# Moving the output gate's products from the stick-breaking heads into the mLSTM heads

## The reference, cut to what matters

```
q_sb, k_sb, v_sb, qk_ml, v_ml, o_ml, i_ml, f_ml = jnp.split(h @ w_in, cuts)
y_sb = rms_norm_2(stick_breaking(q_sb, k_sb, v_sb), g_out_sb)
y_ml = rms_norm_2(mlstm(q_ml, k_ml, v_ml, i_pre, f_pre), g_out_ml) * sigmoid(o_ml)
x = x + gate1 * (concat(y_sb, y_ml) @ w_out)
x = x + gate2 * peer(h2, ...)          # 128 experts per token, gathered rows
```

## Time and profile before

| | |
|---|---|
| median of three runs | 2725.64 us |
| the profiled execution, its time | 2722.03 us |
| its span | 2720.3 us |
| busy PE / DVE / ACT / POOL | 2202.9 / 1785.0 / 632.5 / 786.2 us |
| last values of stick-breaking end, half 0 / half 1 | 754.1 us / 1750.1 us |
| mLSTM from its first matmul to its last result, half 0 / half 1 | 754.9 to 776.2 us / 1750.9 to 1780.7 us |

### The profile page before, as it was taken

How to read it: one execution, slowest core, us unless ns; L and a number is a source line. 1 busy time by engine, 2 the same in 40 slices (tenths; PEclk the granted TensorE clock), 3 DMA queues, 4 the chain that set the end, 5 groups by cost and what they waited for, 6 DMA issues and landing times. The chain is left out here.

```text
span 2720.3 us, 26208 instructions
## 1 busy us (share of the span) xinstructions
PE 2202.9 (81%) x9020; PEld 1638.8 (60%) x9020; DVE 1785.0 (66%) x3684; ACT 632.5 (23%) x1441; POOL 786.2 (29%) x543
## 2 busy tenths in 40 slices
PE   8999999999989999898999997979555545545544
PEld 6787888888768778677788786768111212212211
DVE  4662110003337778687777686767899999999987
ACT  2103212002322420563230125522221111111110
POOL 0000000000000234234433332313754655545552
PEclk9999999999989999899999998989767777777776
DMA  6874334443234699798999874647999999999997
GB/s 250 291 269 142 130 112 153 154 155 124 78 123 182 245 377 399 263 336 330 383 421 420 365 301 178 232 170 272 403 421 407 421 422 422 421 390 421 422 421 312
DMA packets 114868, 798.33 MB, mean 293 GB/s; under 512 B 13328, under 2 KB 16528, under 8 KB 19248
## 3 DMA queue, kind: packets, MB, share of 16 engines
q0 software_dynamic: 74736, 540.57, 49.0%
q1 hardware_dynamic: 40000, 256.08, 25.5%
HBM read 790.27 MB, written 6.33 MB: 293 GB/s over the span
## 5 line engine op out<-in xcount | busy, mean ns | idle before, releaser
L566 PE MATMUL PS<-reg,ring 128*128 128x256 f32 x6016 | 1353.4, 385 | 43.8 <-DVE reg L1484 10.8
L566 PEld LDWEIGHTS PS<-reg,ring 128*128 128x128 f32 x6016 | 1146.9, 193 | 221.9 <-issue 42.4
L517 POOL DMA_INDIRECT uv<-in_expert_uv,experts x318 | 519.4, 1633 | 1590.1 <-DVE experts L1348 859.5
L1395 DVE SCALAR_TENSOR_TENSOR acc<-uv,coef,acc 128x1024 f32<-128x1024 f32 x256 | 328.9, 1285 | 9.1
L544 PE MATMUL PS<-reg,spare 128*128 128x512 f32 x224 | 169.8, 916 | 193.7 <-ACT spare L964 189.7
L1366 DVE CUSTOM_DVE_ANT_0 uv<-uv,h_tok 128x1024 f32<-128x1024 f32 x222 | 263.7, 1219 | 40.1 <-DMA uv<-in_expert_uv,experts 40.0
L544 PEld LDWEIGHTS PS<-reg,spare 128*128 128x128 f32 x224 | 62.8, 297 | 300.0 <-issue 300.0
L544 PE MATMUL PS<-uv,spare 128*128 128x512 f32 x240 | 151.0, 776 | 88.9 <-ACT spare L964 88.9
L971 ACT ACTIVATE acts<-dots 128x2 f32<-128x2 f32 (+2 forms) x194 | 39.5, 203 | 771.0 <-DVE dots L1366 715.2
L517 POOL DMA_INDIRECT reg<-in_expert_uv,experts x114 | 156.8, 1376 | 207.4 <-PE PS L544 152.4
L544 PE MATMUL PS<-ring,spare 128*128 128x512 f32 x152 | 104.8, 839 | 88.9 <-ACT spare L964 85.5
(11 more groups left out here) (255 smaller groups left out, 2200.3 us busy)
## 6 DMA issues: line engine op xcount, KB each, us to landing
ring<-in_weights SPq DMA_DIRECT2D x228, 1024.0 KB
uv<-in_expert_uv,experts POOLq DMA_INDIRECT x318
reg<-in_x_t SPq DMA_DIRECT2D x2, 1024.0 KB, 6.0
kv_half<-reg SPq DMA_DIRECT2D x1, 2048.0 KB, 12.3
reg<-in_sub_t SPq DMA_DIRECT2D x2, 1024.0 KB, 4.8
toep<-rel_neg SPq DMA_DIRECT2D x16, 128.0 KB
x_tokens<-reg SPq DMA_DIRECT2D x2, 1024.0 KB, 10.2
reg<-kv_half SPq DMA_DIRECT2D x1, 2048.0 KB
```

What stands on the lines that cost most here:

```text
L517: gp.indirect_dma_start(UV[r], None, a["expert_uv_2"], bass.IndirectOffsetOnAxis(ap=experts[:, e % 256:e % 256 + 1], axis=0))\
L566: mm = pe.matmul(out_tile(n, t), w[:, t * P:(t + 1) * P], mv, start=first and k == 0, stop=last and k == KT - 1)
L1395: dve.scalar_tensor_tensor(acc[:, :], v, c, acc[:, :], ALU.mult, ALU.add).then_inc(acc_done, 1)
```

## The change

The two VM blocks stay in rounds 0 to 3 of stick-breaking. Rounds 4 to 7 have no product block any more. The four gate tiles are now done in the mLSTM, one for each head e, between the scores of head e+1 and the values of head e. ScalarE takes the tanh straight from PSUM there, and VectorE the x/2+1/2 after the head's result. As H must now live until the last gate tile, the mLSTM's results go to QM, whose query tile of head e has been read when its result is written. Of the eight expert steps of half 1, six stay in stick-breaking (rounds 0 to 4 and 6) and two come after heads 1 and 3 of the mLSTM; rounds 5 and 7 lose also the table load that brings the logarithm's table back.

```diff
         def mixed(m):
-            return QS[:, m, :] if m < 4 else H[:, m - 4, :]
+            return QS[:, m, :] if m < 4 else QM[:, m - 4, :]
...
# TensorE, stick_breaking
-                fill = [weights_block(NO[hf, kind, i], h, token_major=kind == VM) for kind in (VM, OM) for i in range(2)]
+                fill = [weights_block(NO[hf, VM, i], h, token_major=True) for i in range(2)]
...
-                    next(fill[c // 2])
+                    if c < 4:
+                        next(fill[c // 2])
                     values(c)
# TensorE, mlstm
+                fill = [weights_block(NO[hf, OM, i], h) for i in range(2)]
                 scores(0)
                 for e in range(NML):
                     if e + 1 < NML:
                         scores(e + 1)
+                    next(fill[e // 2])
                     values(e)
# ScalarE, stick-breaking
-                    kind, i, t = VM if c < 4 else OM, c // 2 % 2, c % 2
-                    n = NO[hf, kind, i]
-                    tile_wait(act, n, t)
-                    dst = VL[:, t, BW * i:BW * i + BW] if kind == VM else OMT[:, 2 * i + t, :]
-                    act.activation(dst, out_tile(n, t), ACT.Copy).then_inc(evac_sem(n, t), 1)
-                    if t:
-                        tick(hf, kind, i)
-                    elif hf:
+                    i, t = c // 2, c % 2
+                    if c < 4:
+                        n = NO[hf, VM, i]
+                        tile_wait(act, n, t)
+                        act.activation(VL[:, t, BW * i:BW * i + BW], out_tile(n, t), ACT.Copy).then_inc(evac_sem(n, t), 1)
+                    if c < 4 and t:
+                        tick(hf, VM, i)
+                    elif hf and t == 0:
                         owe(1)
                     settle()
-                    if hf and c + 1 < NH2:
+                    if hf and c + 1 < NH2 and (c < 4 or t == 0):
                         ready_for_soft()
-                for j in range(4):
-                    evac_wait(act, NO[hf, OM, j // 2], j % 2)
-                    act.activation(OMT[:, j, :], OMT[:, j, :], ACT.Tanh, scale=0.5).then_inc(om_tanh, 1)
# ScalarE, mLSTM, head e
                         ml_exps(e + 1)
+                    n = NO[hf, OM, e // 2]
+                    tile_wait(act, n, e % 2)
+                    act.activation(OMT[:, e, :], out_tile(n, e % 2), ACT.Tanh, scale=0.5).then_inc(evac_sem(n, e % 2), 1)
+                    settle()
...
+                    if e % 2:
+                        tick(hf, OM, e // 2)
# VectorE, stick-breaking
-                    if c % 2:
-                        tick(hf, VM if c < 4 else OM, c // 2 % 2)
-                    elif hf:
-                        next(experts_dve)
+                    if c % 2 == 0:
+                        if hf:
+                            next(experts_dve)
+                    elif c < 4:
+                        tick(hf, VM, c // 2)
# VectorE, mLSTM
-                for i in range(4):
-                    dve.wait_ge(om_tanh, 4 * hf + i + 1)
-                    dve.tensor_scalar(OMT[:, i, :], OMT[:, i, :], 0.5, 0.5, ALU.mult, ALU.add).then_inc(om_done, 1)
...
                     dve.tensor_tensor(mixed(4 + e), PS[:, 4 + e % 2, 0:T], den, ALU.mult).then_inc(ml_y, 1)
+                    evac_wait(dve, NO[hf, OM, e // 2], e % 2)
+                    dve.tensor_scalar(OMT[:, e, :], OMT[:, e, :], 0.5, 0.5, ALU.mult, ALU.add).then_inc(om_done, 1)
+                    if e % 2:
+                        tick(hf, OM, e // 2)
```

More of the change, by code:

```diff
@@ L327, in build @@
             "silu_done", "ada_acc", "ada_mm", "mod_done", "gain_done"))
-        conv2, tanh_qk, silu_qk, om_tanh, om_done, kv_stored, kv_loaded = (sem(n) for n in (
-            "conv2", "tanh_qk", "silu_qk", "om_tanh", "om_done", "kv_stored", "kv_loaded"))
+        conv2, tanh_qk, silu_qk, om_done, kv_stored, kv_loaded = (sem(n) for n in (
+            "conv2", "tanh_qk", "silu_qk", "om_done", "kv_stored", "kv_loaded"))
         gate_mm, gate_act, gate_row, b_xpose, b_copy = (sem(n) for n in (
@@ L891, in half @@
                         evac_wait(pe, NO[hf, VM, i], t)
-                        evac_wait(pe, NO[hf, OM, i], t)
                 mlstm(hf)
+                for t in range(2):
+                    evac_wait(pe, NO[hf, OM, 1], t)
                 for j in range(4):
@@ L1849, in half @@
                     head_scale(hf, 3, j, 1, mixed(j + 4), col("g_out_ml", j))
+                    dve.wait_ge(om_done, 4 * hf + j + 1)
                     dve.wait_ge(hn_done, 32 * hf + 26 + 2 * j)
```

## The result

The changed kernel takes 2734.39 us (median of 21 runs, 2727.61 to 2740.55) against 2725.26 us before (21 runs, 2717.06 to 2734.45): ratio 1.0038, 95% interval 1.0029 to 1.0047. It is slower, by 9.1 us on the medians, 10 by the ratio. The forecast was 2730 us, between 2721 and 2742, with 58% for "no visible change" and 28% for slower.

What follows compares the result with a forecast made beforehand. TensorE was taken to bound both mixers. Half 0's -1.7 us and half 1's +6.2 sum to +4.5: 2726.5 us on the profiled 2722.03, 2730.1 on the median; 8 in 10 between 2721 and 2742.

Steps and rivals of the forecast that it cites:

- no visible change: Case (A), whole kernel: TensorE's work is conserved, time stays within about 0.3% (8.2 us); chance 58%.
- the step behind head 3: Half 1's mLSTM: this expert step falls into VectorE's 4.59 us wait for the root and adds 0.7 us.
- Half 0's walk: Half 0, stick-breaking rounds 4 to 7: without tiles values 7 end at 742.0 instead of 754.1, -12.1 of 14.2 us.
- the cold spell: Half 0, 758 to 762: clock granted 0.60, mostly at the lower level; +1.5 us taken for it.
- The bound of 1.7 us for the tile: Half 0's mLSTM: the first gate tile loses up to 1.7 us if the low-clock spell falls on it.
- The term of -0.5 for the means: Half 0, behind the mLSTM: a denser mLSTM leaves the means at the high clock for a while, -0.5 us.
- Half 1's waits: Half 1, stick-breaking without tiles: TensorE idles about 7.5 us instead of 0.6, in waits of 2.2, 1.8 and 3.5 us.
- the clock term of half 1: Half 1: a low-clock spell over the mLSTM's first scores after the 3.5 us wait costs 0 to 2.5 us; +1 taken.
- Rival (B): Slower by the clock: gate tiles run at the low level, 3.55 us more each; 2742 with two a half; chance 26%.
- the 75% row: Half 1's mLSTM before the change: TensorE 75% busy at clock 1.00 throughout, taken as evidence against (B).
- (C): Faster: rounds 4 to 7 loop quicker than walked, -6 us in half 0, -4 in half 1, 2716; chance 13%.
- (D): WO2's blocks, requested late, stall TensorE; one stall of 5 to 8 us in half 1 gives 2737; chance 3%.

Runs made afterwards that it cites:

- the pad: The changed kernel with 7 matmuls of no use before values 7 in half 1, where TensorE waits for head 7's Exp; ratio to before 1.0017.
- the pad of 12: The changed kernel with 12 matmuls of no use after the values of head 6 in half 1; they took 5.4 us; ratio to before 1.0027.
- one tile back: The changed kernel with round 6's expert step in the mLSTM's head 0, plus the first gate tile back in round 5 in both halves; ratio 0.9994.
- the late Gelu: The changed kernel with ScalarE's Gelu of round 6's expert step (half 1) after the Exp of head 7 instead of before it; ratio 1.001.
- the step in the mLSTM: The changed kernel with half 1's expert step of round 6 moved into head 0 of the mLSTM; ratio 0.9986, run again 0.9997.

## Why the prediction was right, and where it was off

The range held (2721 to 2742; 2734.4 measured), and half 1 lost as forecast. The point, 2730, was 4.4 us low: the forecast loss of 4.5 us is half of the measured one. Half 0's forecast gain of 1.7 us can't be told from none (0.3 in the profile, ratio 0.9997 alone). The likeliest case, no visible change, did not come: the loss is 0.38%, a little over the bound, and one term was mis-sized.

| us | predicted | measured |
|---|---|---|
| half 0, stick-breaking | -12.1 | -12.2 |
| half 0, mLSTM to its last result, clock in it | +9.4 + 1.5 | +11.9 |
| half 0, behind it | -0.5 | +0.1 |
| half 1, stick-breaking | -7.4 | -5.9 |
| half 1, mLSTM to its last result | +11.9 | +15.5 |
| half 1, the step behind head 3 | +0.7 | +0.8 |
| of half 1, clock | +1 | +5.7 |
| half 1 in all | +6.2 | +10.5 |

(The line on the clock is an addend of its own in the prediction; in what was measured it is the pad's share, already inside the three lines above it. The measured parts are differences of rows: stick-breaking from tile 3 to the last copy, 754.15 - 727.59 before and 745.76 - 731.42 after in half 0, 41.11 and 35.21 in half 1.)

- **Half 0's walk** through stick-breaking was right to 0.1 us: the rounds without a tile give 12 of 14.2 us back, and the mLSTM takes them again. That the cold spell would not go but fall on the first tile was foreseen; in this profile it cost 0.9 us there and more in the scores. The bound of 1.7 us for the tile was too narrow: in five of the eight profiles with this half 0 it took 5.6 to 5.95 us instead of 3.62. The term of -0.5 for the means was an argument without a row, and did not come (+0.1). So the close agreement of half 0 (-1.7 against -0.3) is in part luck: its mixer moves by 2.3 us from one profile to the next.
- **Half 1's waits** came as walked, 2.08, 0.52 and 3.42 us against 2.2, 1.8 and 3.5: only the second was overestimated, and for a reason that the walk did not have: the clock fell behind the first wait, so the sums of head 6 took 1.6 us longer and filled most of the second. The Gelu and two table loads in front of the last Exp were in the walk. Without the clock half 1 was predicted at +5.2 and measured, with the fitting pad, at +4.8.
- **The step that failed is the clock term of half 1**, "costs between 0 and 2.5 us. I take +1". Its bounds came from the earlier trace rows, where TensorE was low for some 6 us and then recovered. Here it was low for nearly 14 us, though busy 10.4 of the last 10.4. The pad shows 5.7 us. With that in the sum the forecast would have been +9.2 us, against +9.1 of the medians.
- **Rival (B)** had the mechanism and the wrong victims. It put the low clock on gate tiles; in half 1 they ran at 3.62 to 3.77 us. It was the mLSTM's own first matmuls, values 7 and the sums of head 6 that were slow. I argued against (B) from the 75% row at 1.00 in the earlier trace rows, since it covers the loop that the tiles go to; but that row had rounds in front of it that were full, and the change thinned exactly these. Its "5.9 busy of 8.2 us" stands in no row shown; by the walk the thinned rounds are busy for some 15.7 of 23.2 us. The Trainium skill, TensorE: Matmul & The Clock Gate, "A second HAM failure mode: psum-queue depth-cycling", says that small idle times between groups of matmuls can let the clock swing. This case's trace agrees in part: in the thinned rounds of half 1 the clock was at 0.69 in one window and 1.00 in those around it, so it did swing, but behind waits of 2.08 and 3.42 us and not behind the one of 0.52, and seven matmuls of no use in the longest kept it up.
- **(C)** did not come: the loop was no quicker than walked. **(D)** did not come: WO2's blocks caused no wait; the last request in half 0 went out at 775.6 instead of 753.7 us and was not missed.
- **The results' place** and the tanh were costed at nothing; the first is shown, the second was only argued from the rows. Two small readings were off and enter no sum: half 1's mixer lies in slices 26 and 27, and TensorE's gap behind half 1's last head was 4.02 us before, so that 3.7 us could be filled there and not 3.3.

## What to carry to other kernels

In this kernel the work that filled TensorE's waits also kept its clock up. Before moving it, walk the round that is left, find its longest wait, and look for small things in front of its releaser: here a 0.2 us activation between two table loads, hidden until then. Price the wait twice, once for itself and once for the clock behind it; in this kernel the second price was the larger, and moving the small thing took back two thirds of what the change had cost (7.0 of 10.5 us of the mixer).

## What the runs showed of the hardware

- After a wait of 3.42 us TensorE's clock was at the lower level for nearly 14 us (granted 0.52 over 13.95 us, busy 13.39); with matmuls of no use in the wait it stayed at the higher one. In both profiles of the change the spell was the same (mixer 95.02 and 95.00 us), and nearly so with half 1 changed alone (94.83).
- After the wait of 2.08 us it was granted 0.50 for 2.7 us. All nine profiles with this wait have the first sums behind it at 1.22 us instead of 0.70; with the gate tile in the wait they took 0.59.
- A long wait is not needed for a spell: with the pad of 12 (first tile 5.02 us), with one tile back (first scores 3.15 us) and in half 0 the clock fell with no wait over 1 us in front. In the kernels with the pad of 7, with the late Gelu and with the step in the mLSTM it stayed up over the same matmuls, behind waits of 0.20 to 1.58 us. So the runs show what took this spell away, and no rule for when one comes.
- In half 0 such a spell is not so steady. Over the kernels whose half 0 is the same code, its mixer took 61.91, 65.52, 62.56 and 64.84 us in the form of before, and 61.65, 61.72, 63.87, 63.86, 61.64, 63.88, 62.43 and 63.96 us in the changed form, the first tile 4.4 to 4.5 us long in the three shortest of these and 5.6 to 5.95 in the others. A single profile can't tell the two forms apart there. What decides the length of such a spell, and why it was so much longer in half 1 than the one before the change, stays open.
- ScalarE's change of table took 1.28 us, and the activation followed 0.02 us behind (1741.14 after 1739.84). The Trainium skill, ScalarE: Activation LUTs, "What ACT_TABLE_LOAD costs", adds a drain of about 1.4 us to each. The rows here differ, and they decide: from the end of the Gelu (1741.34) to the start of the Exp (1742.65), with the table changed between, there are 1.31 us.
